# Two modulation rounds of layer 1 summed on VectorE before one product each, and the shared round moved to the end

## The reference, cut to what matters

```python
mod = jax.nn.silu(c) @ p['ada_w'] + p['ada_b']          # ada_w: 1024 x 6144
mod_c = jax.nn.silu(c_ctx) @ p['ada_w'] + p['ada_b']
sh_a, sc_a, g_a, sh_f, sc_f, g_f = split(mod, 6)        # shift, scale, gate, twice
csh_a, csc_a, cg_a, csh_f, csc_f, cg_f = split(mod_c, 6)
h = modulate(rmsnorm(x, norm_mix), sh_a, sc_a)          # hc likewise with csh_a, csc_a
y, y_c = mixer(h, hc)
x = x + g_a * y
x = x + g_f * peer_ffn(modulate(rmsnorm(x, norm_ffn), sh_f, sc_f))
if need_ctx:                                            # layer 0 only
    xc = xc + cg_a * y_c
    xc = xc + cg_f * peer_ffn(modulate(rmsnorm(xc, norm_ffn), csh_f, csc_f))
```

## Time and profile before

| | |
|---|---|
| time, median of 3 runs | 2360.91 us (2359.05 to 2363.62) |
| the profiled execution | 2362.36 us, its span 2360.6 us |
| busy, share of the span | PE 69%, DVE 66%, POOL 40%, ACT 36% |
| HBM | 924.77 MB in all, mean 392 GB/s |
| mean granted clock of TensorE | 0.843 |

### The profile page before, as it was taken

How to read it: one execution, slowest core, us unless ns; L and a number is a source line. 1 busy time by engine, 2 the same in 40 slices (tenths; PEclk the granted TensorE clock), 3 DMA queues, 4 the chain that set the end, 5 groups by cost and what they waited for, 6 DMA issues and landing times.

```text
span 2360.6 us, 27277 instructions
## 1 busy us (share of the span) xinstructions
PE 1633.6 (69%) x9141; PEld 717.0 (30%) x9141; DVE 1556.4 (66%) x3642; ACT 850.9 (36%) x2538; POOL 946.8 (40%) x840
## 2 busy tenths in 40 slices
PE   7997887768777666758555656569787765545654
PEld 3654543323333223324111211125453311111111
DVE  1226677887766667877767665554867878766654
ACT  2223444435443333443423423233423332332322
POOL 1212344444454344444544444410343644444441
PEclk8999998888988788989777876889998977777677
DMA  9997899999999999999999999982699999999996
GB/s 398 383 365 290 342 391 419 420 421 410 421 413 420 420 420 420 419 420 420 421 419 416 421 421 420 421 344 89 256 393 417 420 421 422 421 422 421 421 421 252
DMA packets 139162, 924.77 MB, mean 392 GB/s; under 512 B 17015, under 2 KB 22935, under 8 KB 32270
## 3 DMA queue, kind: packets, MB, share of 16 engines
q0 software_dynamic: 112816, 807.16, 82.9%
q1 hardware_dynamic: 26062, 115.86, 12.3%
q10 hardware_dynamic: 144, 0.01, 0.0%
HBM read 921.82 MB, written 1.15 MB: 391 GB/s over the span
## 4 chain that ended last, share of the span: by engine, by line
DMA 47%; PE 24%; DVE 16%; issue 5%; ACT 4%; POOL 3%; SPq 0%; POOLq 0%; DVEq 0%; ACTq 0%
DMA arena<-in_uv,small 44%; PE bank L1309 10%; DVE arena L2167 8%; PE bank L754 3%; POOL arena L693 3%; PE bank L719 2%; ACT aux L1562 2%; PE bank L151 1%; PE bank L901 1%; DMA arena<-in_ada 1%; PE bank L740 1%; DVE aux L2089 1%; PE bank L731 1%; PE bank L1185 1%; ACT small L1555 1%
## 5 line engine op out<-in xcount | busy, mean ns | idle before, releaser
L1309 PE MATMUL bank<-arena,aux 64*64 64x512 f32 x6016 | 955.1, 783 | 645.5 <-ACT aux L1562 607.0
L693 POOL DMA_INDIRECT arena<-in_uv,small x764 | 900.0, 1178 | 1204.4 <-PE bank L1309 882.2
L2167 DVE CUSTOM_DVE_ANT_0 arena<-arena,h 128x1024 f32<-128x1024 f32 x764 | 921.1, 1226 | 485.7 <-DMA arena<-in_uv,small 479.4
L1309 PEld LDWEIGHTS bank<-arena,aux 64*64 64x64 f32 x6016 | 272.4, 175 | 1275.5 <-ACT aux L1562 726.3
L1555 ACT ACTIVATE small<-small 128x4 f32<-128x4 f32 (+2 forms) x198 | 40.5, 205 | 1156.8 <-DVE small L2167 1156.7
L1546 ACT ACTIVATE aux<-small 128x64 f32<-128x64 f32 x768 | 204.3, 336 | 11.3 <-DVEq L2158 2.6
L1562 ACT ACTIVATE aux<-aux,small 128x64 f32<-128x64 f32 x768 | 204.9, 336 | 6.8 <-ACT small L1555 0.5
L754 PE MATMUL bank<-hT,aux 128*128 128x256 f32 (+1 forms) x752 | 163.7, 374 | 5.0 <-DMA aux<-in_w_query 2.7
L754 PEld LDWEIGHTS bank<-hT,aux 128*128 128x128 f32 x752 | 134.1, 197 | 48.9 <-issue 28.1
L1518 ACT ACT_TABLE_LOAD x67 | 86.0, 1283 | 1.2
L2167 DVE DVE_READ_ACCUMULATOR2_ANT small<- 128x1 f32 x768 | 63.0, 82 | 0.0
(11 more groups left out here) (265 smaller groups left out, 1575.9 us busy)
## 6 DMA issues: line engine op xcount, KB each, us to landing
arena<-in_ada SPq DMA_DIRECT2D x36, 1024.0 KB, 10.3
aux<-in_w_query SPq DMA_DIRECT2D x43, 512.0 KB, 7.9
arena<-in_uv,small POOLq DMA_INDIRECT x764, 17.5
arena<-in_w_head SPq DMA_DIRECT2D x16, 512.0 KB, 10.1
hT<-in_ada SPq DMA_DIRECT2D x7, 1024.0 KB, 8.6
arena<-in_w_qkv SPq DMA_DIRECT2D x3, 2048.0 KB, 8.8
h<-in_ada SPq DMA_DIRECT2D x5, 1024.0 KB, 12.8
arena<-in_w_o SPq DMA_DIRECT2D x4, 1024.0 KB, 10.1
```

Source lines behind the costliest of these rows:

```text
L693: nc.gpsimd.indirect_dma_start(out=slot_at(pos), out_offset=None, in_=d["uv"][unit // FIRST], in_offset=bass.IndirectOffsetOnAxis(ap=self. ...
L1309: last = nc.tensor.matmul(bank[2 * r + m][out:out + 64, :], self.dg[rr, (s + o) % 8, :], slot_at(at)[rr, cols], start=first, stop=False)
L2167: last = nc.vector.tensor_tensor_reduce(out=slot_at(at)[:, 0:D], in0=slot_at(at)[:, 0:D], in1=h[:, c * D:(c + 1) * D], scale=1.0, scalar=0 ...
```

## The change

Round (1, 0), which both kinds of token need, moves to the end of `ROUNDS`. Rounds (1, 2) and (1, 1), of which only the latents' row is read, are no longer multiplied chunk by chunk: VectorE multiplies each chunk by the latents' column of `cs` (a scalar for each partition) and adds it to a running total that lies in the place of the round's first chunk (`ada_weighted`). TensorE then multiplies the total once (`ada_total`) by a 128 x 2 matrix of a column of ones and a column of zeros, which sums the partitions. Two chunks are summed in each step u from 4 to 8 and one in step 9; the last five (35 to 39) are summed after `norm_rows` of token chunk 0, ahead of the top 16. The places of the chunks from 24 on, the order of loads, the buffers of bias rows, the late gains and all waits are set accordingly. All 8 chunks of the last round are multiplied after the first scores.

```diff
-ROUNDS = ((0, 0), (0, 1), (0, 2), (1, 0), (1, 2), (1, 1))
+ROUNDS = ((0, 0), (0, 1), (0, 2), (1, 2), (1, 1), (1, 0))
+SUMMED = (3, 4)
+    def ada_total(self, bank, weighted, pick):
+        for s in range(NQ):
+            last = self.nc.tensor.matmul(bank[s * Q:s * Q + 2, :], pick, weighted[:, 2 * s:2 * s + 2, :], start=True, stop=True)
+        return last
-        first = (6, 0, 1, 2, 3, 5, 4, 6, 0, 1, 2, 11)
+        first = (6, 0, 1, 2, 3, 4, 5, 6, 0, 1, 2, 11)
         def ada_place(n):
-            if n < 40:
-                return n % 8 if n < 32 else 4 + n % 4
-            return (4, 5, 6, 4, 5, 4, 5, 4)[n - 40]
+            if n < 24:
+                return n % 8
+            return (4, 5, 6, 7, 5, 6, 7, 6, 5, 7, 6, 4, 6, 4, 6, 4, 4, 5, 4, 5, 4, 5, 4, 5)[n - 24]
-        ADA_AFTER = (range(14, 16), range(16, 20), range(20, 24), range(24, 27), range(27, 30), range(30, 32), range(32, 34), range(34, 36),
-                     range(36, 38), range(38, 40))
+        ADA_AFTER = (range(14, 16), range(16, 20), range(20, 24))
+        SUMS_AT = {4: (24, 25), 5: (26, 27), 6: (28, 29), 7: (30, 31), 8: (32, 33), 9: (34,)}
...
                     last = ada_last_use(n)
-                    if last is not None:
-                        sp.wait_ge(ada_used, last + 1)
+                    if last is not None and summed(last) and last % KD:
+                        sp.wait_ge(ada_summed, last - KD * SUMMED[0] + 1)
+                    elif last is not None:
+                        sp.wait_ge(ada_used, ada_count(last + KD - 1 if summed(last) else last))
...
-                for i in range(4):
-                    sp.wait_ge(ada_used, 25 + i)
-                    sp.dma_start(self.w_o_first[:, 2 * i:2 * i + 2, :], ...)
-                    ada(32 + i)
+                    if n >= 24 and n % 2:
+                        i = (n - 24) // 2
+                        sp.wait_ge(ada_used, 17 + i)
+                        sp.dma_start(self.w_o_first[:, 2 * i:2 * i + 2, :], ...)
                 job(0)
-                for n in range(36, 40):
+                for n in range(32, 38):
                     ada(n)
                 sp.wait_ge(kp_done, 7)
                 head(0, True)
                 sp.wait_ge(kp_done, 8)
                 head(1, True)
-                for n in range(40, 43):
-                    ada(n)
                 ...                                     # rope_cols, keys_next
-                for n in range(43, 45):
+                for n in range(38, 40):
                     ada(n)
-                sp.wait_ge(ada_used, 43)
+                sp.wait_ge(ada_summed, 15)
                 ...                                     # wq_next, both sides
-                for n in range(45, steps):
+                for n in range(40, steps):
                     ada(n)
...
+                def ada_sum(r):
+                    pe.wait_ge(cs_zero, 6)
+                    pe.wait_ge(bank_taken, r)
+                    pe.wait_ge(ada_summed, KD * (r - SUMMED[0] + 1))
+                    self.ada_total(bank[0], ada_slot(KD * r), self.lat_pick).then_inc(ada_used, 1)
...
-                    for n in ADA_AFTER[u]:
+                    for n in ADA_AFTER[u] if u < len(ADA_AFTER) else ():
                         ada(n)
+                    if u == 8:
+                        ada_sum(3)
                 out_head(0, H - 1, (bank[4], bank[7]))
-                pe.wait_ge(silu_done, 2)
-                for n in range(40, 43):
-                    ada(n)
                 pe.wait_ge(hf_ready, 1)
                 transposes(0, h, (bank[6], bank[7]), ft_done)
                 pe.wait_ge(ft_copied, 2)
                 first_query(0, 0)
+                ada_sum(4)
                 pe.wait_ge(keys_loaded, 16)
                 pe.wait_ge(q_copied, 1)
                 score(0, self.keys).then_inc(sc_done, 1)
-                for n in range(43, 45):
+                for n in range(40, 42):
                     ada(n)
                 for hd in range(4):
                     out_head(1, hd, (bank[6], bank[7]))
                 first_query(1, 0)
-                for n in range(45, 47):
+                for n in range(42, 44):
                     ada(n)
                 for hd in range(4, H):
                     out_head(1, hd, (bank[6], bank[7]))
                 ...
                 score(1, keys_next).then_inc(sc_done, 1)
-                ada(47)
+                for n in range(44, steps):
+                    ada(n)
...
+                def ada_weighted(n):
+                    k, total, weights = n % KD, ada_slot(n - n % KD), ada_slot(n)
+                    dve.wait_ge(ada_loaded[ada_place(n)], 16 * ada_turn(n))
+                    if k == 0:
+                        nc.vector.tensor_scalar(total, weights, self.cs[:, k, LAT:LAT + 1], None, ALU.mult).then_inc(ada_summed, 1)
+                        return
+                    dve.wait_ge(ada_summed, n - KD * SUMMED[0])
+                    nc.vector.scalar_tensor_tensor(out=total, in0=weights, scalar=self.cs[:, k, LAT:LAT + 1], in1=total,
+                                                   op0=ALU.mult, op1=ALU.add).then_inc(ada_summed, 1)
...
-                        if u == (0, 1, 3, 6)[r]:
+                        if u == (0, 1, 3, 9)[r]:
                             ada_rows(r)
                     ...                                 # rotate, ctx_out
-                ada_rows(LAYERS * ADA_ROUNDS - 2)
+                    for n in SUMS_AT.get(u, ()):
+                        ada_weighted(n)
...
                 norm_rows(0, self.mix_rows[:, 1], self.gate_f, hf_ready)
                 first_mean(1)
+                for n in range(35, 40):
+                    ada_weighted(n)
+                ada_rows(4)
                 dve.wait_ge(sc_done, 1)
                 ...                                     # tops_now, both sides
-                dve.wait_ge(stored, 16 * NQ * (LAYERS * ADA_ROUNDS - 1))
+                dve.wait_ge(stored, 16 * NQ * (LAYERS * ADA_ROUNDS - 2))
                 choose_first(0)
                 first_rstd(1)
                 finish_gates(0)
+                dve.wait_ge(stored, 16 * NQ * (LAYERS * ADA_ROUNDS - 1))
                 dots(0, 0, range(GRP))
                 ada_rows(LAYERS * ADA_ROUNDS - 1)
```

More of the change, by code:

```diff
@@ L279, in trunk @@
         rows_late = self.qk[:, 512:1024]
-        gains = self.aux[:, 2816:3328]
+        gains, gains_late = self.aux[:, 2816:3328], self.qk[:, 1024:1536]
         rope_rows_ctx = v(self.aux, 3328, CC, 2 * ROPE)
@@ L316, in ada_last_use, with ada_count, summed @@
             return max((m for m in range(n) if ada_place(m) == ada_place(n)), default=None)
-        ADA_AFTER = (range(14, 16), range(16, 20), range(20, 24), range(24, 27), range(27, 30), range(30, 32), range(32, 34), range(34, 36),
-                     range(36, 38), range(38, 40))
+        def ada_count(n):
+            return n + 1 - (KD - 1) * sum(1 for r in SUMMED if KD * r <= n)
+        def summed(n):
+            return n // KD in SUMMED
+        ADA_AFTER = (range(14, 16), range(16, 20), range(20, 24))
+        SUMS_AT = {4: (24, 25), 5: (26, 27), 6: (28, 29), 7: (30, 31), 8: (32, 33), 9: (34,)}
         OUT_AFTER = {6: (0, 1), 7: (2, 3), 8: (4, 5), 9: (6,)}
+        ROW_BUFFER, ROW_TURN = (0, 1, 0, 0, 1, 1), (1, 1, 2, 3, 2, 3)
         def rows_of(r):
-            return rows_late if r == len(ROUNDS) - 1 else rows[r % 2]
+            return rows_late if r == len(ROUNDS) - 1 else rows[ROW_BUFFER[r]]
         def ada_turn(n):
@@ L629, in store_rows @@
                         pool.wait_ge(m_done, 1)
-                    if r + 2 < len(ROUNDS) - 1:
-                        self.ada_load_rows(*ROUNDS[r + 2], rows[r % 2], pool, rows_loaded[r % 2])
+                    follows = (2, 4, 3, None, 5)[r]
+                    if follows:
+                        self.ada_load_rows(*ROUNDS[follows], rows_of(follows), pool, rows_loaded[ROW_BUFFER[follows]])
                     if r == len(ROUNDS) - 2:
-                        self.ada_load_rows(*ROUNDS[r + 1], rows_late, pool, rows_loaded[1])
+                        self.ada_load_gains(1, (2, 3), gains_late, pool, gains_loaded)
                     if r == 2:
@@ L684, in _ @@
                     elif pos < 6:
-                        pool.wait_ge(ada_used, max(m for m in range(steps) if ada_place(m) == pos) + 1)
+                        pool.wait_ge(ada_used, ada_count(max(m for m in range(steps) if ada_place(m) == pos)))
                     elif pos == 6:
@@ L1949, in ada_rows @@
                     dve.wait_ge(bank_taken, r + 1)
-                    dve.wait_ge(gains_loaded, 16 * NQ * (layer + 1))
+                    late = r == len(ROUNDS) - 1
+                    dve.wait_ge(gains_loaded, 16 * (NQ * (layer + 1) + 2 * late))
                     first = ((SC_A, None, SC_F)[i] * D - i * ADA) // 512 * Q
                     part = at[first:first + 2 * Q]
```

(6 more changed lines are left out.)

14 lines of the change are left out of this document (9 added, 5 removed).

## The result

The changed kernel takes 2399.22 us (median, 2398.83 to 2402.47) against 2362.26 us for the kernel before: 37.0 us more, ratio 1.016 with a 95% interval of 1.0142 to 1.0177. The forecast was 2384 with a range up to 2396. The direction was right, and most of the places where time was lost; the size was not: 37 us and not 23, 3 us above the range.

The account below looks back on a forecast made before the run. A chain of waits was taken to bound the prologue, and bytes the gathers from 320 us on. Losses of 3.5 us up to `hf_ready` and 19.6 us behind it, 23.1 in all, gave 2384 us, range 2370 to 2396.

Parts of the forecast that it names:

- Steps 3 to 5 give back nothing, and only steps 6 to 9 have products on the path: TensorE, attention steps: copies hide chunk products in steps 3 to 5; steps 6 to 9 each have 1.9 us on the path.
- the bound of 6.6: Steps 6 to 9: at most 6.6 us won from TensorE's removed products, less 0.9 us for the total's product.
- The sums ahead of `normalise`: VectorE, steps 4 to 8: sums of 2.36 us delay `normalise` and TensorE's transposes, turning the gain into about 3.5 us lost.
- The 1.0 us for steps 4 and 5: Steps 4 and 5: sums delay `normalise` and the transposes waiting for it, 0.5 us in step 4, 1.0 us in all.
- upper bound 8: At `hf_ready`: 8 us lost at most, if loads are later than the forecast loss of 3.5 us assumes.
- Behind `hf_ready`: From `hf_ready` (T, ahead of the transposes) to `add_mix(1)`: five sums, few places and late loads lose 19.6 us.
- The clock: Total's product behind `hf_ready`: idle TensorE falls to 1.2 GHz, so it costs 1.9 us and not 0.9.
- made up later: Rival, prologue: idle DMA time absorbs part of the delay; 2372 us if half of 23 us is absorbed; chance 0.15.
- Loads are the new bound: Rival: chunks 33, 37, 39 and 47 each take 10.3 us, 12 to 15 us more, 2396 to 2399; chance 0.11.

Follow-up runs that it names:

- e2: Changed kernel with each step's sums ahead of `rotate` and not behind `ctx_out`; 30.8 us above the kernel before, ratio 1.0129.
- e7: Kernel before, same round order, with chunks 32 to 37 summed by VectorE and a third and fourth place for the last round; 5.0 us less, ratio 0.9981.
- e1: Changed kernel with the weights of context head 7 issued behind chunk 27 and not 29; 37.7 us above the kernel before, ratio 1.0156.
- e8: e2 with only round (1, 2) summed and round (1, 1) multiplied by TensorE again; 27.4 us above the kernel before, ratio 1.0118.
- e5: e2 without the loads of chunks 46 and 47, TensorE multiplying their places' old contents again; 21.5 us above the kernel before, ratio 1.0095.
- e10: e2 with a third place for the last round and chunks 44 and 45 used between out heads; 23.3 us above the kernel before, ratio 1.01.

## Why the prediction was wrong in size

- **Steps 3 to 5 give back nothing, and only steps 6 to 9 have products on the path.** Right. e2 multiplies no chunk in steps 3 to 5, and its scores of step 6 start at 129.69 us for 129.48. e7 takes products only out of steps 6 to 9: its `norm_rows` ends at 162.8 us for 170.1, 7.4 us earlier, where four steps at 1.9 us make 7.5 (the bound of 6.6 counted the total's product in step 8).
- **The sums ahead of `normalise`.** Right: 2.35 us each (2.36 forecast), and a wait of 3.13 us in step 7 (154.39), where the forecast's times for the end of `normalise` and of the scores give 3.2. From the sum of chunk 29 to `add_mix(0)` 21.8 us were forecast and 21.5 measured. The 1.0 us for steps 4 and 5 came out (130.55 for 129.48) by luck. The transposes of step 5 did not wait for VectorE, whose `normalise` ended 2.2 us ahead of them; instead the scores of step 5 took 3.30 us for 1.83, mostly at the lower of the clock's two levels (granted clock 0.73 over 120 to 125 us). TensorE's gap of 2.64 us, no longer filled with products, lies ahead of them; but the same gap stands ahead of the scores of steps 4 and 6, which ran at the full clock (0.67 us for two passes). So such a gap can be followed by the lower clock and is not always.
- **The step that failed ahead of `hf_ready` is a missing one.** I traced what SyncE's waits do to chunk 32 and to `job(0)`, but not to the weights of head 7, which stand in the same queue behind chunk 29. They cost 6.55 us of standing and 2.1 us more for the first work behind it at the lower clock (4.87 us for 2.75), 8.7 us together. Measured loss at `hf_ready` 12.2 us, forecast 3.5, upper bound 8: the difference is these 8.7. That the weights are this term is shown in the traces of e1 (5.4 us back, 7.4 in the step itself) and e2, where earlier sums also free them; in time e1 gained nothing clear of the scatter.
- **Behind `hf_ready`** the mechanism was right, in us from T:

| | forecast | measured |
|---|---|---|
| chunk 37 landed | 7.4 | 7.1 |
| chunk 39 summed | 17.9 | 18.8 |
| top 16 | 21.8 | 23.5 |
| first gather | 30.3 | 32.6 |
| chunk 41 used | 26.2 | 29.0 |
| chunk 43 used | 38.9 | 43.2 |
| chunk 45 used | 48.6 | 52.6 |
| chunk 47 used | 56.6 | 63.6 |
| `add_mix(1)` | 58.0 | 65.2 |

Three terms were too small. Chunk 41 was taken to land right behind chunk 40, but its place is that of the round's total (chunk 32), so it could be issued only when the total was multiplied, and it landed at 28.0. The first four out heads took 8.83 us and not 7.13, at the lower clock again. Chunk 47 landed 9.0 us after its issue at 235.4 and not 7.1, and TensorE had waited 7.10 us for chunk 46 ahead of it.
- **The clock.** For the total's product I took 1.9 us, and the trace has 1.89, behind 9.60 us of idling and at a granted clock of 0.50 (1.2 GHz). It has 1.04 us for the same product in step 8, behind work and at a granted clock of 1.00 (2.4 GHz). The Trainium skill ("TensorE: Matmul & The Clock Gate", Part 1) has an idle TensorE fall to 1.2 GHz and return to 2.4 GHz with sustained work; these two products agree. By its Part 3 the column tile follows from where the output starts in PSUM; the trace agrees, since eight passes took 1.04 us and not 3.60. I counted the lower clock for one product, where it also touched the scores of step 5, the projections of head 7 and the first out heads.
- **Rivals.** Nothing is made up later: the share behind `add_mix(1)` is unchanged, and the time followed `add_mix(1)` in every kernel of the table. "Loads are the new bound" was the nearest rival, with 2396 to 2399 and a chance of 0.11, but its mechanism is not what happened: chunks 33, 37, 39 and 47 took 8.9, 4.8, 6.9 and 9.0 us, none the 10.3 that it assumed. The queue and the places made the difference.
- **How the loss divides.** Of 39 us, 12 to 13 lie ahead of `hf_ready` (e2). Behind it, as rough shares from kernels that differ in more than one thing, summing the second round costs 6 us in the trace and 3 in time (e8 against e2), and the wait for the last two chunks in two places 10 (e5). Some 10 of the 26.8 us stay for the rest of the last round behind the scores; no run takes them apart, and e10 gave back 3 of them with a third place and another order.

## What to carry to other kernels

When a load's buffer is handed to another engine, list everything behind that load on the same queue, and ask for each when it is wanted, not only for the loads that the change is about. Work moved to an idle engine is free where nothing waits for it: the same sums cost 13 us behind `ctx_out`, with the loads that wait for them, and nothing ahead of `rotate` (e2), while e7 has four of its six sums behind `ctx_out` in steps 7 to 9 and loses nothing that shows. And find the point on which the saturated stream depends (here the last chunk's product and what follows it, not the first gather) and give it buffers first.

## What the runs showed of the hardware

The first sum of a round, a `tensor_scalar` from SBUF to SBUF on 128x2048 float32, takes 1.28 us, where I had estimated 1.6 to 2.0; the sum with a second tensor takes 2.35. The Trainium skill ("VectorE: DVE Perf Modes", the section on mode 2×_2P) says that a single-source operation in SBUF runs at two float32 elements per cycle and one with a second tensor does not; the trace agrees, with a ratio of 1.84. A 1 MB chunk landed 4.7 to 4.8 us after its issue with nothing ahead of it (in the chains of the changed kernel, e2 and e6), and 9.0 us with another chunk ahead of it and gathers beside it (chunk 47 of the changed kernel).
